# Hybrid encoder layer step on one core: the feed-forward output product by two groups of token tiles instead of two column halves

## The reference, cut to what matters

```python
def swiglu(h, w_in, w_out):
    gate, up = jnp.split(h @ w_in, 2, axis=-1)
    return (jax.nn.silu(gate) * up) @ w_out          # w_out: (2816, 1024)

def residual(x, out, g, gate, weight):
    return x + weight * gate[:, None, :] * rms_norm(out, g)

x = residual(x, swiglu(modulate(x, ...), w_ffn1_in, w_ffn1_out), g_norm[1], mod[:, 2], 0.5)
heads, new_state = mixer(modulate(x, ...))
x = residual(x, heads @ w_out, ...)
x = residual(x, swiglu(modulate(x, ...), w_ffn2_in, w_ffn2_out), g_norm[5], mod[:, 8], 0.5)
```

## Time and profile before

| what | value |
|---|---|
| time, median of 3 runs (lowest, highest) | 1456.66 us (1452.57, 1461.25) |
| the profiled execution | 1456.57 us |
| its span in the trace | 1454.8 us |
| PE busy | 91% |
| DVE, ACT, POOL busy | 57%, 39%, 22% |
| DMA | 152.71 MB, mean 105 GB/s |
| the stage `ffn_out(0)` | 360.6 to 525 us |
| the stage `ffn_out(1)` | 1289.6 to 1443 us |

### The profile page before, as it was taken

How to read it: one execution, slowest core, us unless ns; L and a number is a source line. 1 busy time by engine, 2 the same in 40 slices (tenths; PEclk the granted TensorE clock), 3 DMA queues, 4 the chain that set the end, 5 groups by cost and what they waited for, 6 DMA issues and landing times.

```text
span 1454.8 us, 23707 instructions
## 1 busy us (share of the span) xinstructions
PE 1330.3 (91%) x8072; PEld 1155.8 (79%) x8072; DVE 825.3 (57%) x1445; ACT 571.9 (39%) x1131; POOL 321.4 (22%) x276
## 2 busy tenths in 40 slices
PE   4999999999999969999996678987999999999996
PEld 2889999998778849888874345766899999988885
DVE  2666777666345464424245755238677777754545
ACT  4533443433244364232112446337344444433433
POOL 0443343432000000000101604004344444410000
PEclk9999999999999989999956578998999999999998
DMA  9545444553523323212210405002332222212232
GB/s 316 158 146 161 147 153 144 157 153 115 173 95 108 119 66 102 88 58 101 87 32 21 139 13 175 18 23 92 87 87 81 77 73 86 87 55 75 87 136 109
DMA packets 167003, 152.71 MB, mean 105 GB/s; under 512 B 10361, under 2 KB 139777, under 8 KB 166954
## 3 DMA queue, kind: packets, MB, share of 16 engines
q1 hardware_dynamic: 165610, 148.24, 32.4%
q0 software_dynamic: 1344, 3.81, 1.0%
HBM read 142.72 MB, written 9.05 MB: 104 GB/s over the span
## 4 chain that ended last, share of the span: by engine, by line
PE 79%; DVE 9%; issue 5%; ACT 4%; DMA 2%; DVEq 0%; SPq 0%; POOL 0%; ACTq 0%; POOLq 0%
PE ps L1079 75%; DVE resid L1941 1%; DVE h_sums_lo L1722 1%; DVE max_den L2216 1%; DMA resid<-in_x_sample 1%; DVE w_sums_lo L1722 1%; DMA w_raw<-in_w_ffn_in 1%; ACT probs L995 1%; DVE w_lo L1722 1%; DVE act_t L1833 1%; PE ps L1605 1%; DVE silu_gate L1826 1%; ACT x_norm L661 1%; DVE probs L2225 1%; DVE y L1904 0%
## 5 line engine op out<-in xcount | busy, mean ns | idle before, releaser
L1079 PE MATMUL ps<-h_sums_hi,w_sums_hi 128*128 128x320 f32 x1216 | 378.2, 315 | 15.2 <-ACT silu_gate L731 4.5
L1079 PE MATMUL ps<-h_sums_hi,w_sums_lo 128*128 128x320 f32 x1216 | 371.1, 309 | 0.0
L1079 PE MATMUL ps<-h_sums_lo,w_sums_hi 128*128 128x320 f32 x1216 | 371.0, 309 | 0.0
L1079 PEld LDWEIGHTS ps<-h_sums_hi,w_sums_hi 128*128 128x128 f32 x1216 | 227.1, 188 | 31.9 <-issue 20.8
L1722 DVE TENSOR_TENSOR w_lo<-w_raw,w_hi 128x512 fp32r<-128x512 f32 (+3 forms) x106 | 97.8, 923 | 232.3 <-ACT w_hi L805 157.7
L1079 PEld LDWEIGHTS ps<-h_sums_hi,w_sums_lo 128*128 128x128 f32 x1216 | 227.5, 188 | 0.0
L1079 PEld LDWEIGHTS ps<-h_sums_lo,w_sums_hi 128*128 128x128 f32 x1216 | 227.5, 188 | 0.0
L1079 PE MATMUL ps<-w_hi,act_hi 128*128 128x512 f32 x440 | 174.7, 397 | 4.3 <-issue 3.6
L1079 PE MATMUL ps<-w_hi,act_lo 128*128 128x512 f32 x440 | 172.6, 392 | 0.0
L1079 PE MATMUL ps<-w_lo,act_hi 128*128 128x512 f32 x440 | 172.5, 392 | 0.0
L1722 DVE TENSOR_TENSOR w_sums_lo<-w_raw,w_sums_hi 128x512 fp32r<-128x512 f32 x136 | 126.5, 935 | 54.3 <-ACT w_sums_hi L749 44.4
(11 more groups left out here) (325 smaller groups left out, 1919.1 us busy)
## 6 DMA issues: line engine op xcount, KB each, us to landing
w_raw<-in_w_ffn_in SPq DMA_DIRECT2D x88, 512.0 KB, 3.8
w_raw<-in_w_ada SPq DMA_DIRECT2D x28, 1024.0 KB, 5.1
w_raw<-in_w_ffn_out SPq DMA_DIRECT2D x88, 256.0 KB, 2.6
w_raw<-in_w_in SPq DMA_DIRECT2D x10, 1024.0 KB, 5.1
w_raw_start<-in_w_ada SPq DMA_DIRECT2D x8, 1024.0 KB, 7.8
w_raw<-in_w_out SPq DMA_DIRECT2D x4, 1024.0 KB, 5.0
k_cache<-in_cache_k SPq DMA_DIRECT2D x8, 512.0 KB, 4.9
v_cache<-in_cache_v SPq DMA_DIRECT2D x8, 512.0 KB, 3.8
```

The lines of the kernel that those rows point to most:

```text
L1079: return pe.matmul(out, lhsT, rhs, start=start, stop=stop)
```

## The change

The product is still done in two passes over the 22 inner tiles, but a pass now takes a group of token tiles and both column halves: group 0 is the tiles 0, 1, 2 (six banks), group 1 the tiles 3, 4 (four banks). Each load is 128 rows of all 1024 columns, and the weights' high and low parts are 1024 columns wide; the activations' parts are those of the group alone, 384 or 256 columns. A step is done product by product over the banks, not bank by bank, with a wait ahead of each product for its own part; the last step of a group waits for all parts and goes bank by bank. The squares, gating, mean, root, residual addition and (f = 0) the norm of group 0's rows are put between the turns of group 1 on ScalarE and VectorE; only group 1's two tiles are left for behind the stage. The residual's tiles are loaded back in the last five turns of group 0. The gate's transposes use banks 5 and 7 in two pairs. ScalarE's first high part waits for the sixth of the last seven products. `residual(0)`, `residual(2)` and `norm_rows(1)` go.

```diff
         def out_view(T, s):
-            return T[:, 0, s * 1024:s * 1024 + 512]
+            return T[:, 0, s * 1024:(s + 1) * 1024]
+        OUT_TILES = ((0, 1, 2), (3, 4))
+        OUT_COLS = (slice(0, 3 * P), slice(3 * P, TOK))
+        def out_bank(t, half):
+            return (0, 1, 2, 3, 4, 6, 5, 7, 0, 1)[2 * t + half]
+        def gate_bank(r, j):
+            return 5 + j % 3 if r == 1 else (5, 7)[j % 2]
...
-                            sp.dma_start(out_view(RAW, s), ffn_out[f][bass.ds((2 * t + s) * P, P), half * 512:(half + 1) * 512]).then_inc(k_landed[s], 16)
+                            sp.dma_start(out_view(RAW, s), ffn_out[f][bass.ds((2 * t + s) * P, P), :]).then_inc(k_landed[s], 16)
...
+                    if half == 0:
                         sp.wait_ge(f_act, (f + 1) * FT)
                         if f:
                             sp.wait_ge(x_spilled, 16 * NT)
-                        for t in range(NT + 2):
+                        for t in range(ADA_OUT, OUT_TURNS):
                             turn(t)
-                            if t >= 2:
...
+                            tile = t - ADA_OUT
+                            if tile < NT:
...
-                act.wait_ge(f_p, 7 * (f + 1) * REG + 4 * (f + 1) - 6)
-                out_hi(0, 0, 2 * f * OUT_TURNS)
+                act.wait_ge(f_p, 7 * (f + 1) * REG + 4 * (f + 1) - 1)
+                out_hi(0, 0, 2 * f * OUT_TURNS, 0)
...
                 act.wait_ge(k_landed[s], 16 * (n + 1))
                 act.wait_ge(k_mm[s], n)
-                act.activation(WH[:, 0, s * 1024:s * 1024 + 512], RAW[:, 0, s * 1024:s * 1024 + 512], ACT.Copy).then_inc(k_hi[s], 1)
-                act.activation(ASTH[:, s, :], ACTT[:, bass.ds(2 * t + s, 1), :].rearrange("p a n -> p (a n)"), ACT.Copy).then_inc(k_hi[s], 1)
+                act.activation(out_view(WH, s), out_view(RAW, s), ACT.Copy).then_inc(k_hi[s], 1)
+                cols = OUT_COLS[group]
+                act.activation(ASTH[:, s, cols], ACTT[:, bass.ds(2 * t + s, 1), cols].rearrange("p a n -> p (a n)"), ACT.Copy).then_inc(k_hi[s], 1)
...
+                out_hi(0, 0, n1, 1)
+                tile_squares(f, 0)
+                tile_squares(f, 1)
+                out_hi(1, 0, n1, 1)
+                tile_squares(f, 2)
+                for t in range(1, OUT_TURNS):
                     for s in range(2):
-                        out_hi(s, t, n0 + t)
+                        out_hi(s, t, n1 + t, 1)
+                    if t == 2:
+                        y_root(2 * f, 0, slice(0, 3))
+                    if f == 0 and 5 <= t < 8:
...
+                        row_squares(t - 5)
+                    if f == 0 and t == 8:
+                        row_root(0, slice(0, 3))
                 roots_table()
-                y_squares(2 * f, 1, out_bank(f, 1))
+                tile_squares(f, 3)
+                tile_squares(f, 4)
+                y_root(2 * f, 1, slice(3, 5))
+                if f == 0:
+                    for t in (3, 4):
+                        row_squares(t)
+                    row_root(1, slice(3, 5))
+                    act.wait_ge(x_rstd, rows_roots(1, 1))
+                    act.activation(XN[:, 4, :], X[:, 4, :], ACT.Copy, scale=RS[:, 0, 4:5]).then_inc(x_norm, 1)
...
+            def out_parts(s, n, i):
+                if i == 0:
+                    pe.wait_ge(k_hi[s], 2 * (n + 1))
+                else:
+                    pe.wait_ge(k_lo[s], 2 * n + i)
+            def out_mm(s, n, group, start=False, free=None):
+                for i in range(3):
+                    out_parts(s, n, i)
+                    for t in OUT_TILES[group]:
+                        for half in range(2):
+                            if free and i == 0:
+                                free(t, half)
+                            q = out_tile(s, n, group, (i,), start, False, t, half)
+                return q
+            def out_last(n, group):
+                for i in range(3):
+                    out_parts(1, n, i)
+                for t in OUT_TILES[group]:
+                    for half in range(2):
+                        q = out_tile(1, n, group, range(3), False, True, t, half)
...
+                        if group and t == 3 and half == 0:
+                            pe.wait_ge(gate_rows, 8 * f + 4)
+                        elif group and t == 4:
+                            pe.wait_ge(y_copied, 4 * NT * f + half + 1)
+                        elif not group and t == 0:
+                            if half:
+                                pe.wait_ge(f_up, 7 * (f + 1) * REG)
+                                pe.wait_ge(f_act, (f + 1) * FT)
+                            else:
+                                pe.wait_ge(f_cp, (f + 1) * REG)
...
+                out_lo(0, 0, n1, 1)
+                tile_gated(r, 0)
+                tile_gated(r, 1)
+                out_lo(1, 0, n1, 1)
+                tile_gated(r, 2)
+                for t in range(1, OUT_TURNS):
                     for s in range(2):
-                        out_lo(s, t, n0 + t)
-                y_gated(2 * f, 1)
+                        out_lo(s, t, n1 + t, 1)
+                    if t == 1:
+                        inverse_mean(1, slice(0, 3), y_sq, y_count(r, 2, 1), y_ms)
+                    if 3 <= t < 6:
+                        if t == 3:
+                            dve.wait_ge(y_rstd, roots(r, 0))
+                        add_tile(r, t - 3)
+                    if f == 0 and t == 7:
+                        inverse_mean(0, slice(0, 3), x_sq, NT + 3, x_ms)
+                    if f == 0 and t >= 8:
+                        norm_row(t - 8, 0)
+                tile_gated(r, 3)
+                tile_gated(r, 4)
+                inverse_mean(1, slice(3, 5), y_sq, y_count(r, 4, 1), y_ms)
+                dve.wait_ge(y_rstd, roots(r, 1))
+                for t in (3, 4):
+                    add_tile(r, t)
+                if f == 0:
+                    inverse_mean(0, slice(3, 5), x_sq, 2 * NT, x_ms)
+                    norm_row(3, 1)
```

More of the change, by code:

```diff
@@ L1073, in _ @@
             ffn_out(1)
-            residual(2)
         @block.tensor
@@ new lines, in out_last, with free @@
+            def out_last(n, group):
+                for i in range(3):
+                    out_parts(1, n, i)
+                for t in OUT_TILES[group]:
+                    for half in range(2):
+                        q = out_tile(1, n, group, range(3), False, True, t, half)
+                        if not (t == OUT_TILES[group][-1] and half):
+                            q.then_inc(out_done, 1)
+                q.then_inc(k_mm[1], 1)
+            def ffn_out(f):
+                for group in range(2):
+                    n0 = (2 * f + group) * OUT_TURNS
+                    def free(t, half):
+                        if group and t == 3 and half == 0:
[6 more added lines that the diff above has]
+                                pe.wait_ge(f_act, (f + 1) * FT)
+                            else:
+                                pe.wait_ge(f_cp, (f + 1) * REG)
@@ L1272, in with_ada @@
                     def with_ada(n, start=False):
-                        out_mm(0, n, start=start, before=free if start else None).then_inc(k_mm[0], 1)
+                        out_mm(0, n, group, start, free if start else None).then_inc(k_mm[0], 1)
                         ada_mm(FT + n)
-                        out_mm(1, n).then_inc(k_mm[1], 1)
+                        out_mm(1, n, group).then_inc(k_mm[1], 1)
                         ada_tr(FT + n)
```

185 lines of the change are left out of this document (93 added, 92 removed).

## The result

| | median | lowest to highest | runs |
|---|---|---|---|
| before | 1454.12 us | 1449.35 to 1461.25 | 11 |
| changed | 1468.12 us | 1457.29 to 1478.98 | 11 |
| profiled execution of the changed kernel | 1457.65 us | | |

The ratio is 1.0086, 95% interval 1.0049 to 1.0123: slower, as forecast. (It goes by the means; the two medians are 14.0 us apart, 0.96%.) The kernel before came out 2.5 us lower with 11 runs than with the three of the prediction. Two things in this table need an explanation of their own: the changed kernel's runs scatter over 21.7 us where the kernel before has 11.9, and the profiled execution is nearly the quickest of its runs, only 1.1 us above that of before. So the whole spans are not to be compared; the stages are.

A forecast was written before the change was run, and what follows sets the result against it. TensorE's matmul line, 75% of the chain of waits, was taken as the bound. Loop 19.2, handover 0.8, tails -4.7 and -3.6, modulation's loads -0.3 sum to +11.4 on 1456.57: 1468.0 us, range 1457 to 1477.

The forecast's parts named there:

- The slot's loop in the second group: Output product, second group: a 6.37 us load-and-split round against TensorE's 5.45 makes TensorE wait; 19.2 us lost over both stages.
- the modulation: First stage's six turns with the modulation's loads: the weight load takes longer but TensorE needs it 1.4 us later; -0.3 us.
- The work between the turns at nothing: Additions, squares and root moved between second-group turns fit gaps on VectorE and ScalarE; cost nothing, at most 9 us without cover.
- The tails: Behind each output stage: three fewer additions, and less normalizing in the first; -4.7 us in the first, -3.6 in the last.
- The handover: From feed-forward input to output: VectorE's last product stands behind a longer low part; 0.4 us per stage, 0.8 for both.
- The clock: Second group's step gaps, under 1 us: expected to leave the granted clock up, like an earlier 0.7 us stall at 1.00.
- The sum: Whole kernel: 19.2 + 0.8 - 4.7 - 3.6 - 0.3 = +11.4 us, giving 1468.0 us.
- (1) the load arrives in time: Second group's load comes early enough, so only the tails show: -7.8 us, 1449 us; chance 0.10.
- (2) a quick load: Second group's load lands in 2.7 to 3.05 us: -0.6 to +6.4 us, 1456 to 1463; chance 0.17.
- (3) starved first group: First group's loads, behind the modulation's, each come 1 us late: 5 us more, 1473; chance 0.08 together with the clock rival (4).
- (4) the clock: Clock falls once per output stage: 1.6 us a stage, 1471; in each turn, 30 more; chance 0.08 together with (3).

The follow-up runs named there:

- the buffers: Changed kernel with two load buffers per slot in the second group, each with its own landing semaphore: 1447.96 us, 0.9959 against the kernel before.
- `changed` of the first set: The changed kernel unaltered, run again beside the first set of follow-ups: 1462.44 us, ratio 1.0069 against the kernel before.
- the pair with the swap: Changed kernel and kernel before, both with two low parts exchanged in the feed-forward input stage so one load is issued earlier: 1467.92 and 1457.57 us.
- the kernel before with the swap: Kernel before the change, with the second slot's last low part written ahead of another in the feed-forward input stage: 1457.57 us, ratio 1.0020.
- early load: Changed kernel, but a load waits only for the weights' low part, no longer for the activations' low part: 1454.33 us, 1.0009 against the kernel before.
- half the bytes: Changed kernel, but each second-group load transfers only the first 512 columns, 256 KB: 1459.35 us, ratio 1.0038 against the kernel before.
- the profile with 302.6 us: Changed kernel with two load buffers per slot, loads waiting only for weights' low parts, and last activation product ahead of first low parts: 1449.95 us, 0.9971.
- tails put back: Changed kernel with the first group's mean, root, residual additions and row norm back behind the stage: 1485.28 us, 1.0207 against the kernel before.

## Why the prediction was right, step by step

- **The slot's loop in the second group.** It is the cause, shown by the buffers: with the landing out of the loop 14.5 us go. Its size was 4.5 us too high, and this is the term of the sum that was mis-sized. The forecast had 6.37 us a round; the trace has 6.11, of which the landing is 3.2 to 3.3 (3.3 forecast), issue 0.22 (0.24), the high part 1.07, and the low ones 1.23 and 0.34 instead of 1.28 and 0.42. Ten rounds a stage are so worth 6.6 us, not 9.2. From the first matmul that goes on to the last one, the stages grew by 7.3 and 7.4 us where neither side has a fall of the clock, 14.7 in both, for 19.2 forecast less 0.3 for the modulation. (In the table above it is 5.5 and 9.3: there the kernel before has one fall in each stage, the changed one none in the first and two in the second.) By the Trainium skill (DMA: Bandwidth & Descriptors, Anatomy of one DMA), whose figure is for the other way of issuing, the load was estimated at 3.2 us; the trace has a median of 3.2.
- **The work between the turns at nothing.** Right: taken out again, it leaves the rounds at 6.16 and 6.11 us.
- **The tails.** First stage -4.7, as forecast to 0.1 us. Second -4.0 for -3.6. Put back, they cost 7.5 to 8.5 us at one level of the runs and 9.7 in the trace.
- **The handover.** 0.7 us a stage for 0.4; undone in part it gives 1.0 back. The mechanism was the one named, VectorE's product behind a longer low part; the size was low, as the price of the first low part counts in full there (1.22 us against 0.68).
- **The clock.** It did not fall in the gaps of the second group up to its last step (1.00 over 433 to 528 us), as forecast. Around the longer waits it was not foreseen, and the length of the wait does not decide it: see the last section. A fall costs 2.1 us in the first stage and 1.6 in the second (the kernel before with and without it). The last load's delay by the outputs was not foreseen either; it is there in `changed` of the first set too (3.96 us, and a wait of 2.44), but without a fall.
- **The sum.** +11.4 forecast. The stages show 14.7 + 1.4 - 8.7, about +7.5, and the runs on the lower level are 7.2 us above the kernel before. The line through the clocks says 11.4 and the pair with the swap 10.4 and 12.9, but the first adds 4.2 us for a clock that differs and the pair's profiles differ by three falls. So the direction and the mechanism were right and the size was high by up to 4 us. That the median came out at 1468.12 for a forecast of 1468.0 is luck: the baseline was 2.5 us too high, and 6 of the 11 runs had another 12 us in the second input stage, which no step of the prediction has. It said of that stage nothing at all.
- **Rivals.** (1) the load arrives in time: no, 17 waits for it. (2) a quick load: no, 3.2 us. (3) starved first group: no, TensorE is never idle there from 361 to 441 us; its rounds are 8.16 us in the second stage, TensorE's own, and some 10 in the turns of the first in which TensorE does the modulation's products between. (4) the clock: not in the steps' gaps, but behind waits of 1.6 us and more in some executions.

## What to carry to other kernels

A stage that is bound by TensorE with one buffer per slot has a slack equal to the step's work less the round trip of the slot. A change that makes the step shorter or the load longer spends it, and beyond that point each round costs the difference: write the loop out (issue, landing, each elementwise part) before regrouping, and bring the second buffer along with the change. Set run times of one kernel against their granted clocks before comparing medians: two levels show up that way which a median hides, and whose place can be a stage that the change never touched. Do not read the distance between two kernels off such a line alone, as their clocks may differ too; here it said 11.4 us where the stages, compared without falls of the clock, said 7.5.

## What the runs showed that was not expected

- An input stage with the same code has two patterns, 12.7 and 13.4 us a turn. They go with whether GpSimd's last sum runs beside VectorE's activation product, 0.48 us alone and 1.58 beside it. The slow one lasted through all 19 turns in three profiles and ended after 3 turns (early load) and after 13 (half the bytes) in others. In the kernel before none of 67 runs lies near the upper level (two are 4.7 and 7.2 us over the line), in the changed one 10 of 27 do, but unevenly: 6 of 11, 1 of 10 and 3 of 6 in the result's runs and the two sets. What in the change opens the way to it is not settled, and a part of the chip in it was not ruled out: no run was left to vary the stage's start. The 20 runs of the early load and of the two buffers stayed below the upper level, but in the set where `changed` had it once in ten; and two buffers do not prevent it, as the profile with 302.6 us shows.
- Stores issued behind the last load delay it: 3.9 to 4.1 us for 3.2 in every profile of a 512 KB load with three 512 KB outputs behind it, the first 0.4 to 0.6 us later. Where the outputs come only behind the stage (tails put back), the last load takes 3.25.
- The same wait in the same kernel left the clock up or brought it down. The wait of 2.00 us at the first stage's start left it at 1.00 in the first two profiles of the changed kernel, and a fall followed in the third; 1.62 us brought 0.54 before and no fall in the kernel before with the swap; behind 2.24 us in the last step it was 0.50, behind 2.44 in another run 1.00. The length of the wait alone doesn't tell.
